# Out-projection pieces of two panels placed in the delta rule's waits, its accumulators in the auxiliary banks, and gates by 24 columns

## What is computed

```python
proj = h @ w_in[l]
u_pool, q, k, v, z, a, bt, xr, gr = jnp.split(proj, cuts, axis=-1)
y_pool = pool_mixer(u_pool, ...)                  # 512 columns of the mix
y_gdn  = gated_deltanet(q, k, v, z, a, bt, ...)   # 768 columns, 6 heads, chunks of 64 tokens
y_lru  = rglru_mixer(xr, gr, ...)                 # 768 columns
mixed = jnp.concatenate([y_pool, y_gdn, y_lru], axis=-1)
x = x + mixed @ w_out[l]                          # the out-projection, 2048 x 2048
```

## Time and profile before

| what | value |
|---|---|
| median of three executions | 2094.57 us |
| the profiled execution, its own time | 2092.1 us |
| its span (first to last instruction) | 2090.1 us |
| TensorE busy in the span | 2071.5 us |
| VectorE, ScalarE, GpSimd busy | 1313.8, 961.8, 129.4 us |
| stretch of the middle, Gram products to the third piece | 1137.59 to 1205.27 us |
| out-projection of the second block ends, next panel begins | about 1292 us |

### The profile page before, as it was taken

The page is one execution under the profiler, slowest core; times in us unless marked ns, Lnnn a source line. Parts: engine busy times, 40 slices in busy tenths (PEclk is TensorE's granted clock), DMA queues, the critical chain, the costliest instruction groups (busy, mean ns, idle before and its releaser), DMA issues.

```text
span 2090.1 us, 28025 instructions
## 1 busy us (share of the span) xinstructions
PE 2071.5 (99%) x11271; PEld 1796.3 (86%) x11271; DVE 1313.8 (63%) x1400; ACT 961.8 (46%) x1013; POOL 129.4 (6%) x83
## 2 busy tenths in 40 slices
PE   9999999999999999999999999999999999999998
PEld 8888888888888888888888878888888888888887
DVE  6666656565556557567788655776546764467655
ACT  6444445444444446544667344355333443343433
POOL 0000000000011000030001100012100121000210
PEclk9999999999999999999999999999999999999999
DMA  9755555666656657545554145556565555555553
GB/s 343 241 182 182 181 163 189 195 182 190 189 174 187 186 170 249 194 152 175 168 183 153 41 154 197 193 183 195 188 200 183 192 190 191 191 189 194 182 200 121
DMA packets 318029, 387.36 MB, mean 185 GB/s; under 512 B 9354, under 2 KB 251483, under 8 KB 317659
## 3 DMA queue, kind: packets, MB, share of 16 engines
q1 hardware_dynamic: 309499, 373.93, 55.6%
q10 hardware_dynamic: 8416, 11.78, 1.6%
HBM read 383.58 MB, written 4.69 MB: 186 GB/s over the span
## 4 chain that ended last, share of the span: by engine, by line
PE 97%; DVE 2%; ACT 1%; issue 0%; DMA 0%; DVEq 0%; ACTq 0%
PE acc L1796 39%; PE acc L1806 21%; PE acc L1859 8%; PE acc L1854 8%; PE acc L1855 8%; PE acc L1769 2%; PE acc L1768 2%; PE acc L1773 2%; PE aux L1961 1%; PE aux L1987 1%; PE aux L1972 1%; PE aux L1887 1%; PE aux L2182 0%; PE acc L1737 0%; PE acc L1741 0%
## 5 line engine op out<-in xcount | busy, mean ns | idle before, releaser
L957 DVE TENSOR_TENSOR w_lo<-raw,w_hi 128x2048 fp32r<-128x2048 f32 x343 | 795.2, 2319 | 540.2 <-ACT w_hi L465 539.6
L465 ACT ACTIVATE w_hi<-raw 128x2048 fp32r<-128x2048 f32 (+2 forms) x351 | 663.2, 1890 | 668.5 <-PE acc L1806 313.7
L1796 PE MATMUL acc<-act_x,w_hi 128*128 128x512 f32 x2112 | 510.9, 394 | 0.3 <-ACT w_hi L465 0.3
L1796 PEld LDWEIGHTS acc<-act_x,w_hi 128*128 128x128 f32 x2112 | 390.2, 188 | 77.4 <-issue 0.4
L1796 PE MATMUL acc<-ff_x,w_hi 128*128 128x512 f32 x1536 | 366.6, 391 | 0.0
L1796 PEld LDWEIGHTS acc<-ff_x,w_hi 128*128 128x128 f32 x1536 | 282.4, 188 | 54.7
L1806 PEld LDWEIGHTS acc<-act_x,w_lo 128*128 128x128 f32 x2112 | 270.6, 191 | 10.0
L1806 PE MATMUL acc<-act_x,w_lo 128*128 128x256 f32 x2112 | 274.7, 283 | 0.0
L1806 PEld LDWEIGHTS acc<-ff_x,w_lo 128*128 128x128 f32 x1536 | 196.9, 191 | 7.5
L1806 PE MATMUL acc<-ff_x,w_lo 128*128 128x256 f32 x1536 | 199.4, 283 | 0.0
L1854 PE MATMUL acc<-w_hi,act_x 128*128 128x512 f32 x464 | 181.9, 392 | 2.7 <-DVE act_x L1448 2.7
(11 more groups left out here) (334 smaller groups left out, 1773.9 us busy)
## 6 DMA issues: line engine op xcount, KB each, us to landing
raw<-in_ffn_up SPq DMA_DIRECT2D x96, 1024.0 KB, 5.1
raw<-in_w_in_c SPq DMA_DIRECT2D x64, 1024.0 KB, 5.7
raw<-in_w_in_ab SPq DMA_DIRECT2D x49, 1024.0 KB, 5.1
raw<-in_ffn_down SPq DMA_DIRECT2D x48, 1024.0 KB, 5.0
raw<-in_w_in SPq DMA_DIRECT2D x40, 1024.0 KB, 5.3
raw<-in_w_out_ab SPq DMA_DIRECT2D x16, 1024.0 KB, 5.1
raw<-in_w_out_c SPq DMA_DIRECT2D x16, 1024.0 KB, 5.2
raw<-in_w_out SPq DMA_DIRECT2D x16, 1024.0 KB, 5.0
```

The lines of the kernel that those rows point to most:

```text
L465: copy = lambda out, in_, **k: nc.scalar.activation(out, in_, ACT.Copy, **k)
L957: tt(w_lo[:, c % 2], raw[:, c], w_hi[:, c % 2].bitcast(F32), ALU.subtract).then_inc(lo_ready, 1)
L1796: mm(out(j), wide(w_hi[:, c % 2])[:, k, j * P:(j + 1) * P], x[:, 8 * r + k, :, :].rearrange("p a s -> p (a s)"), start=(r == 0 and k == 0) ...
```

## The change

The pieces of the first two out-panels are fetched and used in another order, `OUT2_PIECES`: pool and LRU pieces of panel 0, then of panel 1, then the delta rule's two pieces of panel 0 and of panel 1. All four pieces of the first kind (96 matmuls) now stand in `middle`, in other places than the two of before. Panel 1 accumulates in `acc[:, 1]`, so the products of the two chunks and the last transposes use `aux` banks. Splits of weights and of the LRU's activations move between engines and places. `out2` does the rest of both panels, and `deproject` begins at the third. VectorE adds panel 0 to the residual during panel 1's first delta piece. The gates use one weight block of 24 columns (high and low) against `act_hi` and the 12 high columns against `act_lo`; the two 12-row halves are added by a product with `fold_gates` in place of the transposes.

```diff
+OUT2_PIECES = ((0, 0), (0, 1), (1, 0), (1, 1), (0, 2), (0, 3), (1, 2), (1, 3))
-        u_bank, carry_bank = acc[:, 1, :], aux[:, 0:2, :].rearrange("p b n -> p (b n)")
-        norm_bank = lambda j: aux[:, 3, :] if j == 2 else acc[:, 1, j * PANEL:(j + 1) * PANEL]
+        u_bank, carry_bank = (aux[:, b:b + 2, :].rearrange("p b n -> p (b n)") for b in (2, 0))
+        norm_bank = lambda j: aux[:, (3, 0, 1)[j], :]
-        x_bank = lambda g: (aux[:, 3, :], acc_bank(3), aux[:, 2, :])[g]
+        x_bank = lambda g: (acc_bank(3), aux[:, 2, :], aux[:, 3, :])[g]
-        v_bank = lambda g: acc_bank((1, 0, 2)[g])
+        v_bank = lambda g: (aux[:, 2, :], aux[:, 3, :], acc_bank(2))[g]
# SyncE
+            for half in range(2):
+                load(AT_OUT2 + half, lambda c: raw[:, c], lambda c: out2_piece(*OUT2_PIECES[4 * half + c]))
+            with sp.Fori(2, N_OUT) as q:
+                load(q + AT_OUT2, lambda c: raw[:, c], lambda c: out2_piece(q, c))
# ScalarE, middle
-                for g in range(3):
-                    beta_values(g)
+                beta_values(0)
+                beta_values(1)
+                split(AT_OUT2, 2)
+                beta_values(2)
...
-                split(AT_OUT2, 2)
+                split(AT_OUT2, 3)
                 for j in range(3):
                     act.wait_ge(go_ready, j + 1)
...
                 f(go_norm, go_norm, ACT.Sqrt, bias=eps).then_inc(go_root, 1)
+                split(AT_OUT2 + 1, 0)
                 for j in range(3):
                     act.wait_ge(go_y, j + 1)
                     copy(act_hi[:, POOL_G + 2 * j:POOL_G + 2 * j + 2, :], tiles(K0 + 2 * j, 2)).then_inc(mid_hi, 1)
+                split(AT_OUT2 + 1, 1)
# VectorE, out_panels, mixers and middle
+                    def before(c):
+                        if c == 1 and i == 1 and paired_up:
+                            dve.wait_ge(w_used, 4 * (gp0 + 1) + 2)
+                            out(0)
+                    tt(fold_gates, ident[0:24, 0:12], ident[0:24, 12:24], ALU.add)
-                for g in range(3):
-                    pack(g)
+                pack(0)
+                pack(1)
                 dve.wait_ge(w_used, 4 * AT_OUT2)
                 to_tile(4 * IN2_PANELS[N_IN2 - 1], 1, LOW_IN2 + N_IN2 - 1)
+                pack(2)
-                better(FIRST_ROUND, amid=lambda: low_of(tiles(XR0, LRU_B), POOL_G + GDN_H, LRU_B))
+                better(FIRST_ROUND, amid=lambda: half_split(2, 0))
+                better(FIRST_ROUND + 1, amid=lambda: half_split(2, 2).then_inc(lo_ready, 1))
-                split(AT_OUT2, 2)
+                split(AT_OUT2, 3)
...
                 low_part(2)
+                split(AT_OUT2 + 1, 0)
+                split(AT_OUT2 + 1, 1)
# GpSimd
             pack_mask(1)
+            pool.wait_ge(mid_hi, 2)
+            lru_low(2, LRU_B)
             pack_mask(2)
...
+                if r == FIRST_ROUND:
+                    lru_low(0, 2)
# TensorE, gates
-                        mm(aux[0:12, 0, 0:S], w_h, act_hi[:, k, :], start=(k == 0), stop=False)
-                        mm(aux[0:12, 0, 0:S], w_h, act_lo[:, k, :], start=False, stop=False)
-                        ins = mm(aux[0:12, 0, 0:S], w_l, act_hi[:, k, :], start=False, stop=(k == NK - 1))
+                        mm(aux[0:24, 0, 0:S], gw[:, k, :], act_hi[:, k, :], start=(k == 0), stop=False,
+                           skip_group_check=True)
+                        ins = mm(aux[0:12, 0, 0:S], gw_hi[:, k, :], act_lo[:, k, :], start=False, stop=(k == NK - 1),
+                                 skip_group_check=True)
...
-                        ins = nc.tensor.transpose(aux[:, 0, S + 12 * t:S + 12 * t + 12],
-                                                  gates_t[:, t * P:(t + 1) * P], ident[0:12, 0:12])
+                        ins = mm(aux[:, 0, S + 12 * t:S + 12 * t + 12], gates_t[:, t * P:(t + 1) * P], fold_gates,
+                                 start=True, stop=True)
# TensorE, middle: out_parts(at, first, end) does the parts first to end - 1 of piece OUT2_PIECES[at]
                 pe.wait_ge(evacuated, 2 * AT_OUT2 - 1)
+                out_parts(0, 0, 4)
                 pe.wait_ge(silu_done, 4)
+                pe.wait_ge(gram_masked, GDN_H)
                 turn_values(0)
                 turn_values(1)
-                pe.wait_ge(gram_masked, GDN_H)
+                out_parts(0, 4, 6)
                 pe.wait_ge(packed_rows, 3)
...
                 turn_values(2)
+                out_parts(1, 0, 3)
                 pe.wait_ge(gv_ready, 2)
-                for part in range(4):
-                    out_part(0, part)
                 for g in range(3):
                     turn_inverse(g)
...                     # the rounds of the inverse
-                out_part(0, 4)
-                out_part(0, 5)
+                out_parts(1, 3, 6)
...                     # u
-                out_part(1, 0)
+                out_parts(2, 0, 1)
...                     # carry
-                out_part(1, 1)
+                out_parts(2, 1, 3)
...                     # u again
-                out_part(1, 2)
+                out_parts(2, 3, 4)
...                     # outputs
-                for part in range(3, 6):
-                    out_part(1, part)
+                out_parts(2, 4, 6)
+                out_parts(3, 0, 2)
...                     # transposes back
+                out_parts(3, 2, 6)
+            def out2():
+                for at in range(4, 7):
+                    out_parts(at, 0, 6)
+                turn_summed(3, AT_OUT2, 0)
+                out_parts(7, 0, 6)
+                deproject(AT_OUT2, N_OUT, act_hi, act_lo, between=turning(3, AT_OUT2), order=OUT2_ORDER, first=2)
```

More of the change, by code:

```diff
@@ L493, in panel, with out_panel @@
                         between(c)
-            def out_panel(gp, between=None, last=False, begun=False):
+            def out_panel(gp, between=None, last=False, begun=0):
                 for c in range(4):
-                    if c < 2:
-                        if not (begun and c == 0):
-                            split(gp, c + 2)
+                    if c < begun:
+                        pass
+                    elif c < 2:
+                        split(gp, c + 2)
                     elif not last:
@@ L540, in summed_squares, with sum_into @@
                     squares_f(i)
-            def sum_into(k, gp0, gain=None, x_hi=None, also=None, last=False, begun=False):
+            def sum_into(k, gp0, gain=None, x_hi=None, also=None, last=False, begun=0):
                 for i in range(N_OUT):
@@ L552, in between @@
                             also(i, c)
-                    out_panel(gp0 + i, between, last=last and i == N_OUT - 1, begun=begun and i == 0)
+                    out_panel(gp0 + i, between, last=last and i == N_OUT - 1, begun=0 if i else begun)
                 if x_hi is not None:
@@ L660, in mixers @@
                     act.wait_ge(gates_mm, 1)
-                    copy(gates_t, aux[0:12, 0, 0:S]).then_inc(gates_out, 1)
+                    copy(gates_t, aux[0:24, 0, 0:S]).then_inc(gates_out, 1)
                 if (p, c) == (1, 2):
@@ L976, in panel, with out_panel @@
                         between(c)
-            def out_panel(gp, out, between=None, last=False, begun=False, before=None):
+            def out_panel(gp, out, between=None, last=False, begun=0, before=None):
                 for c in range(4):
@@ L1085, in low_of_x, with out_panels @@
                 ins.then_inc(lo_act, 1)
-            def out_panels(k, gp0, out, gain, x_hi, x_lo, begun=False):
-                for i in range(N_OUT):
+            def out_panels(k, gp0, out, gain, x_hi, x_lo, paired_up=False):
+                for i in range(1 if paired_up else 0, N_OUT):
+                    def before(c):
+                        if c == 1 and i == 1 and paired_up:
+                            dve.wait_ge(w_used, 4 * (gp0 + 1) + 2)
+                            out(0)
                     def between(c):
@@ L1092, in between @@
                             low_of_x(k, i - 1, gain, x_hi, x_lo)
-                    out_panel(gp0 + i, lambda: out(i), between, begun=begun and i == 0)
+                    out_panel(gp0 + i, lambda: out(i), between, before=before)
                 low_of_x(k, N_OUT - 1, gain, x_hi, x_lo)
@@ L1691, in pack_mask, with lru_low @@
                    const(M_BELOW).unsqueeze(1).broadcast_to([P, 4, P]), mul).then_inc(pack_masked, 1)
+            def lru_low(first, end):
+                hi = act_hi[:, POOL_G + GDN_H + first:POOL_G + GDN_H + end, :].bitcast(F32)
+                tt(act_lo[:, POOL_G + GDN_H + first:POOL_G + GDN_H + end, :], tiles(XR0 + first, end - first), hi, sub
+                   ).then_inc(pool_split, 1)
             pack_mask(0)
@@ L1832, in out_part, with out_parts, deproject @@
                         for t in range(NT):
-                            ins = mm(out(t), x(act_hi, k, t), w_lo[:, c, k, :], start=False, stop=False)
```

(15 more changed lines are left out.)

66 lines of the change are left out of this document (32 added, 34 removed).

## The result

The changed kernel takes 2080.69 us (median of six executions, 2080.66 to 2080.82); the kernel before, in six, 2091.9 (2091.05 to 2094.84). The ratio is 0.9943, 95% interval 0.9930 to 0.9956: 11.2 us less. The profiled executions agree: 2080.8 against 2092.1 us, spans 2078.8 against 2090.1, 11.3 us less. The forecast was 2081.8 us, 12.8 less.

What follows compares the result with a forecast made beforehand. TensorE was taken as the bound, busy 2071.5 of 2090.1 us. Gains of 11.1 us in the middle and 1.7 at the gates, 12.8 together, against the median 2094.57 gave 2081.8 us, range 2079 to 2086.

Steps and rivals of the forecast that it cites:

- The low clock: TensorE at 1.2 GHz right behind the 3.9 and 2.65 us waits; each stretch costs about 1.6 us, both would go.
- The rival by the rule on transposes: Transposes don't count as activity, so a low clock stays; one stretch costs 1.6 us, two 3.2; chance 0.12.
- The chain of the chunks, parts 2 and 3: Rounds, then the chunks' products up to the fifth piece: rounds unchanged at 22.32 us, fifth piece begins at 1206.84.
- Part 1: Gram products to the rounds: 36 piece matmuls instead of 16, rounds begin at 1160.0 instead of 1160.16.
- what GpSimd costs VectorE: Contention before the rounds, GpSimd working beside VectorE's steps: between nothing and 1.64 us, taken as 0.4.
- No wait is left: Ahead of the spread rows: TensorE no longer waits for VectorE's third packing, 0.3 us or so to spare.
- The SBUF page's rule: Shared read path: each blocked inverse step waits up to one GpSimd operation of some 1.2 us, once; sum 0.8 smaller.
- Gates: In-projection's gates: 32 matmuls instead of 48, fold products cost at most 0.2; gain 1.7 us, from 1.4 to 1.85.
- Feeding: Splits and transfers for pieces 4 to 7 come in time behind the middle; cost zero.
- The cover of 1.5 us: VectorE's low split for the pieces behind the middle is done at 1209.0, needed at 1210.5.
- The sum: Whole kernel: 11.1 us from the middle plus 1.7 from the in-projection's gates, 12.8 us less; chance 0.71.

## Why the prediction held, and where it was off

- *The low clock* (predicted 1.6 for each of two stretches): right. When only the idling was filled, 3.1 for both by the profiled executions and 2.4 by the medians; 1.6 for one when it was put back; 1.00 in every stretch shown of the changed kernel. The rival by the rule on transposes did not happen: the clock stayed full through twelve of them at 1201.24. By the Trainium skill ("TensorE: Matmul & The Clock Gate", "Part 4: PE-mode transpose") it might have fallen; these runs can't contradict the rule itself, since large matmuls stand on both sides.
- *The chain of the chunks, parts 2 and 3*: right, in size too. From the rounds' begin to the fifth piece the forecast had 46.84 us (1160.0 to 1206.84), the trace 46.66 (1159.94 to 1206.60).
- *Part 1* failed in one term, what GpSimd costs VectorE. The rounds were put at 1160.0 less the gates' gain; with the gates' real 1.41 this is 1158.6, and they began at 1159.94: 1.35 late. The step was "Bounds: nothing, or one operation's 1.64. I take 0.4." Measured: 1.04 on the copy and 0.84 on the first step of the inverse, together 1.9, 1.5 more than I took and more than the upper bound; 1.35 arrived. I had not looked for the copy at all. "No wait is left" was wrong with it: the third packing ended 1.16 late (1152.36 for 1151.20), and TensorE waited 0.84 for it, where I had asked for under 0.5. The held step then put the inverse behind the spread rows' end by 1.02 instead of 0.31. Moving the copy gave about 1.05 back. The SBUF page's rule, quoted for the inverse ("SBUF — State Buffer", "Who interferes with whom", the Trainium skill), was the better guide: two-input instructions were held (1.08 for 0.24; 2.04 for 0.72), packings, with one input, hardly (1.10 each against 1.06, and GpSimd worked beside them in both kernels). The rule as I quoted it does not cover the copy, which has one input; that it was held is known from its rows alone.
- *Gates* (1.7): the matmuls gave what was worked out, 915.73 to 919.44, 3.71 for 5.47, or 1.76. The fold products cost 0.32 (0.54 to the matmul behind them for 0.22), where I had put at most 0.2: each plain float32 product is two records. That leaves 1.44; the matmuls behind begin 1.41 earlier (925.63 for 927.04), and the run without the edit is 1.3 slower by the medians and 1.4 by the spans.
- *Feeding*: right. ScalarE's split of piece 4 was done at 1201.8, VectorE's at about 1208.7, needed at 1210.22. The cover of 1.5 us was there.
- *The sum*: 1.4 + 9.9 = 11.3 for 12.8. Put together from the measured terms: waits of 3.9, 2.65, 0.81 and 0.74 gone and 0.84 and 0.82 new, 6.4; low clock about 3.1; gates 1.4; the 0.4 left over is about what tails between kinds of matmuls would give, and was not measured by itself.
- *The absolute time* came out 1.1 below the forecast, and that closeness is in part luck. The forecast gain was 1.6 too large, but the base, the median 2094.57 of three executions, was 2.7 too high; over more executions the kernel before has medians of 2091.3 to 2091.9. The two errors have opposite signs.

## What to carry to other kernels

Where TensorE bounds a kernel, look at the granted clock behind each long wait, and price the wait with the slow matmuls behind it. Here waits of 2.65 and 3.9 us, each behind transposes, brought a stretch at half clock, and waits of up to 1.13 us did not; what lies between was not measured. Filling the two waits with useless matmuls, which saves nothing of the waits themselves, still returned 1.2 to 1.5 us for each. When work moves to GpSimd, list every VectorE instruction that can fall into its span, small copies too, since one can be held until the GpSimd instruction beside it ends (a 0.20 us copy took 1.24, a 0.72 us product 2.04); a reordering that frees two can catch a third. Independent matmuls are best cut to the size of each wait, until the chain of the other engines, not TensorE, ends the stretch.

## What the runs showed that I had not expected

- A VectorE copy of 96 columns, 0.20 us alone, took 1.24 beside a GpSimd subtraction, ending 0.07 us after it.
- The kernels with low-clock stretches scatter, the others don't: 2090.18 to 2094.84 for the kernel before and 2084.93 to 2086.51 with the one wait put back, against 0.05 to 0.44 us between lowest and highest for each of the eight kernels whose trace has no low clock ahead of the last microseconds. With the one wait put back the scatter is one execution, 2086.51; the other seven lie within 0.43 us. That the scatter comes from how the stretch falls on the matmuls was not tried.
